# A hybrid decoder layer with its activations kept channel-major, norms accumulated under the matmuls, and interleaved query tiles

## The reference

```python
a = rmsnorm(x, in_norm_g)
u, q, kc, vc, ks, vs, kw, vw, gates = split(a @ w_in)       # 1024, 1024, 6 x 256, 24 columns
q, kc, ks, kw = partial_rope(...)                           # first 32 of 128 head dims
y_pool = (trailing means over 2/4/8/16 tokens - u) @ pool_w * pool_scale
y_nsa = g0 * compressed_attention + g1 * selected_blocks + g2 * window_512
h = x + concat(y_pool, y_nsa) @ w_out
h = h + (silu(n(h) @ w_gate) * (n(h) @ w_up)) @ w_down      # width 5632
h = h + sigmoid(n(h) @ w_ple_gate) * (p @ w_ple_proj)
out = rmsnorm(h, final_norm_g)
```

## Time and profile before

| | us |
|---|---|
| median of 4 runs | 2118.09 (2095.25 to 2284.78) |
| the profiled execution | 2096.27, its span 2094.7 |
| TensorE busy | 1758.5 (84%) |
| VectorE / ScalarE / GpSimd busy | 642.9 / 454.7 / 65.9 |
| DMA | 159 MB moved, 76 GB/s over the span |

### The profile page before, as it was taken

One profiled execution on the slowest core, in us unless ns is written; L12 is line 12 of the kernel. 1 busy time (PEld: TensorE's weight loads), 2 busy tenths in 40 slices (PEclk: granted clock), 3 DMA queues, 4 the chain that ended last, 5 costly groups with the idle time before them and its releaser, 6 DMA issues.

```text
span 2094.7 us, 28609 instructions; the slowest of 8 cores (2078.4 to 2094.7 us)
## 1 busy us (share of the span) xinstructions
PE 1758.5 (84%) x10432; PEld 964.9 (46%) x10580; DVE 642.9 (31%) x1626; ACT 454.7 (22%) x788; POOL 65.9 (3%) x120
## 2 busy tenths in 40 slices
PE   1892999676777784987999999999999999995991
PEld 1782788333444451434444444444444444443440
DVE  2423543151666651224101211131102201135334
ACT  3323212130576670014000000000000000005113
POOL 0000000011000000000000000000000000000000
PEclk9995899885899996997999999999999999995996
DMA  8448233411000007613461633354451526035223
GB/s 217 129 71 190 52 62 62 71 31 32 1 2 1 2 1 175 167 25 76 81 116 25 120 62 69 73 100 82 81 101 31 111 43 129 14 56 131 46 46 160
DMA packets 23033, 159.35 MB, mean 76 GB/s; under 512 B 3696, under 2 KB 5104, under 8 KB 6256
## 3 DMA queue, kind: packets, MB, share of 16 engines
q0 software_dynamic: 15696, 118.00, 30.4%
q1 hardware_dynamic: 7200, 39.51, 5.4%
HBM read 267.12 MB, written 8.39 MB: 132 GB/s over the span
## 4 chain that ended last, share of the span: by engine, by line
PE 78%; DVE 8%; DMA 7%; issue 4%; ACT 3%; DVEq 0%; SPq 0%; POOL 0%; ACTq 0%; POOLq 0%
PE ps L937 14%; PE ps L940 14%; PE ps L953 14%; PE ps L434 11%; PE ps L872 5%; PE ps L1001 5%; PE ps L542 3%; DMA arena<-x 2%; PE ps L720 2%; PE ps L711 2%; DMA arena<-wU 2%; PE ps L708 1%; PE ps L646 1%; DVE arena L910 1%; DVE arena L686 1%
## 5 line engine op out<-in xcount | busy, mean ns | idle before, releaser
L937 PE MATMUL ps<-arena 128*128 128x512 bf16 x1380 | 317.4, 380 | 1.6 <-issue 0.2
L940 PE MATMUL ps<-arena 128*128 128x512 bf16 x1380 | 316.1, 379 | 1.5
L953 PE MATMUL ps<-arena 128*128 128x512 bf16 x1379 | 303.0, 379 | 1.5
L434 PE MATMUL ps<-arena 128*128 128x256 bf16 x2048 | 239.2, 274 | 0.0
L944 DVE TENSOR_TENSOR arena<-ps,arena 128x512 bf16<-128x512 f32 x88 | 60.9, 692 | 548.2 <-PE ps L937 325.5
L943 ACT ACTIVATE arena<-ps 128x512 f32<-128x512 f32 x88 | 52.5, 597 | 782.6 <-PE ps L937 686.5
L937 PEld LDWEIGHTS ps<-arena 128*128 128x128 bf16 x1408 | 138.1, 98 | 166.9 <-issue 1.7
L940 PEld LDWEIGHTS ps<-arena 128*128 128x128 bf16 x1408 | 137.8, 98 | 166.1
L953 PEld LDWEIGHTS ps<-arena 128*128 128x128 bf16 x1408 | 137.7, 98 | 166.2
L434 PEld LDWEIGHTS ps<-arena 128*128 128x128 bf16 x2048 | 196.1, 98 | 23.9
L713 ACT ACTIVATE arena<-ps 128x512 bf16<-128x512 f32 x280 | 161.7, 597 | 85.7 <-PE ps L720 54.9
(11 more groups left out here) (139 smaller groups left out, 1157.9 us busy)
## 6 DMA issues: line engine op xcount, KB each, us to landing
arena<-x SPq DMA_DIRECT2D x24, 1024.0 KB, 12.4
arena<-wdown POOLq DMA_DIRECT2D x16, 1536.0 KB, 15.7
arena<-wgate POOLq DMA_DIRECT2D x22, 1024.0 KB, 9.1
arena<-wup POOLq DMA_DIRECT2D x22, 1024.0 KB, 11.9
arena<-wT POOLq DMA_DIRECT2D x16, 1024.0 KB, 9.5
arena<-wU POOLq DMA_DIRECT2D x8, 1024.0 KB, 10.7
arena<-wout POOLq DMA_DIRECT2D x4, 2048.0 KB, 17.9
arena<-wpg POOLq DMA_DIRECT2D x4, 2048.0 KB, 13.7
```

The costliest lines, as they stand in the source:

```text
L434: PE(lambda e, dc=dc: e.matmul(ps[pbank][:, 0:256], lhsT=aT[:, dc, i * 128:(i + 1) * 128], rhs=wsl[wi][:, dc, :], start=(dc == 0), stop=(d ...
L937: PE(lambda e, dc=dc, sl=sl, half=half, th2=th2, pg=pg: e.matmul(ps[pg][:], lhsT=wgu[sl][:, dc, half * 128:(half + 1) * 128], rhs=a2T[:, d ...
L940: PE(lambda e, dc=dc, sl=sl, half=half, th2=th2, pu=pu: e.matmul(ps[pu][:], lhsT=wgu[sl + 1][:, dc, half * 128:(half + 1) * 128], rhs=a2T[ ...
L953: PE(lambda e, ci=ci, ot=ot, sl=sl, pb=pb, ncq=ncq: e.matmul(ps[pb][:], lhsT=hT[:, ci, ot * 128:(ot + 1) * 128], rhs=wdn[sl][:, ci, :], st ...
```

## The change

The kernel is written anew around the same matmuls.

- Layout: `x`, `p` and the output are handed over channel-major, so channels are on the partitions from the start. The norm's sum over channels is then a sum over partitions: `stat` squares each 128-channel chunk on ScalarE and adds it up on VectorE, `rs` sums over partitions with one float32 matmul by a matrix of 1/2048 and takes the power -1/2 as Exp(-0.5 Ln), `scaled` multiplies. No norm has a transpose.
- Tokens: a core's own tiles are every other tile of the sequence (`OWN`, the odd ones in its numbering) instead of one half; the other core of the sequence has the rest. Local tile 0 is padding on one of the two.
- Projections run over four blocks of 512 tokens (two of other tiles, two of own). All six K and V slabs stay in SBUF (`wkv`). K is projected channel-major and needs no transpose; rotary is done on channel-major data. The norm of block b + 1 is interleaved as `tasks` with the chunks of block b. Q follows for the two own blocks, still held in `aT`.
- Compression: its weights are loaded during the projections, and ScalarE copies K and V into an order in which the stride becomes contiguous (`relay`), one copy after each chunk of Q. Pooling: the halo of 16 tokens is now needed at each tile (128 columns for each channel chunk).
- Attention: a chain at own tile `ot` has 2 `ot` + 2 steps of the selected branch and 2, 4 or 5 of the window; the chains go by `ot`, both groups after each other. The mask matmul and the choice of blocks are left out for `ot` < 4. Masking by `wvalid` goes. All four slots of `wout` are loaded during attention.
- The residual is channel-major. The statistics of the next norm are accumulated in the loops that finish it, and the norm of the first half of the tokens is emitted after the second half's first group. FFN quarters are 12, 12, 12 and 8 chunks.

The core of the diff:

```diff
-        hgs = [4, 5, 6, 7, 8, 9] if pas == 0 else list(range(10))
...
-            ltq = 8 + ot
...
+OTHER = np.arange(0, 16, 2)
+OWN = np.arange(1, 16, 2)
+ORDER = np.concatenate([OTHER, OWN])
...
+            gt = _tiles(th)[ORDER]
+            xl = np.zeros((16, 128, 2048), F)
+            xl[gt >= 0] = x[b].reshape(16, 128, 2048)[gt[gt >= 0]]
+            m["x"] = _c(xl.reshape(4, 512, 16, 128).transpose(0, 3, 2, 1).reshape(4, 128, 16 * 512))
...
+    def stat(src, B_src, i, first, hold=False):
+        a, Ba = acc[i]
...
+        q, Bq = sq[sqr()]
+        ACT(lambda e: e.activation(out=q, in_=src, func=AF.Square), [B_src], [Bq])
+        flush(i)
+        late[i] = lambda: DVE(lambda e: e.tensor_tensor(out=a, in0=a, in1=q, op=ALU.add), [Ba, Bq], [Ba])
...
+    def rs(i, pb):
+        flush(i)
+        a, Ba = acc[i]
+        r, Br = rsb[i]
+        PE(lambda e: e.matmul(ps[pb][:], lhsT=ones, rhs=a, start=True, stop=True), [B_ones, Ba], [PB[pb]])
+        ACT(lambda e: e.activation(out=r, in_=ps[pb][:], func=AF.Ln, bias=eps), [PB[pb], B_eps], [Br])
+        ACT(lambda e: e.activation(out=r, in_=r, func=AF.Exp, scale=-0.5), [Br], [Br])
+
+    def scaled(dst, B_dst, src, B_src, which, dc, i):
+        DVE(lambda e: e.scalar_tensor_tensor(out=dst, in0=src, scalar=gv[:, which, dc:dc + 1], in1=rsb[i][0], op0=ALU.mult, op1=ALU.mult),
+            [B_src, B_gv, rsb[i][1]], [B_dst])
...
         for dc in range(16):
+            tasks.append(lambda dc=dc: stat(*src(dc), b % 2, dc == 0))
+        tasks.append(lambda: rs(b % 2, bank()))
+        for dc in range(16):
+            tasks.append(lambda dc=dc: scaled(aT[b % 2][:, dc, :], B_aT[b % 2][dc], *src(dc), 0, dc, b % 2))
...
+        ACT(lambda e: e.activation(out=dst[64:128], in_=src[64:128].rearrange("p (a b) -> p a b", a=4), func=AF.Copy), [PB[pb]], B_dst)
+        DVE(lambda e: e.tensor_tensor(out=u1[0:64], in0=src[0:64], in1=tab[0:64, 0, :], op=ALU.mult), [PB[pb], Bt], [B1])
+        DVE(lambda e: e.tensor_tensor(out=u2[0:16], in0=src[32:48], in1=tab[32:48, 1, :], op=ALU.mult), [PB[pb], Bt], [B2])
+        DVE(lambda e: e.tensor_tensor(out=u2[32:48], in0=src[0:16], in1=tab[0:16, 1, :], op=ALU.mult), [PB[pb], Bt], [B2])
+        DVE(lambda e: e.tensor_tensor(out=dst[0:64], in0=u1[0:64].rearrange("p (a b) -> p a b", a=4), in1=u2[0:64].rearrange("p (a b) -> p a b", a=4), op=ALU.add),
+            [B1, B2], B_dst)
...
+    for t in x_tasks(0):
+        t()
+    for b in range(4):
+        tasks = x_tasks(b + 1) if b < 3 else []
+        n_done = 0
+        steps = [lambda i=i, t=t: v_chunk(b, t, i) for i in (4, 5) for t in range(4)]
+        steps += [lambda i=i, g=g: kv_chunk(b, i, g) for i in (1, 0, 2, 3) for g in range(2)]
+        upto = [1, 3, 5, 7, 9, 11, 13, 15, 16, 20, 24, 28, 31, 99, 99, 99]
+        for k, f in enumerate(steps):
+            f()
+            while len(tasks) > 0 and n_done < upto[k]:
+                tasks.pop(0)()
+                n_done += 1
...
+                    ACT(lambda e: e.activation(out=cP[k][:, g, :].rearrange("p (h n) -> p h n", h=16)[:, :, n * 32:(n + 1) * 32],
+                                               in_=cT[k][:, g, n * 512:(n + 1) * 512].rearrange("p (n h) -> p h n", h=16), func=AF.Copy), [B_cT[k]], [B_cP[k]])
+                relay.append(piece)
...
+        mm(pb, ps[pb][:, 0:254].rearrange("p (g n) -> p g n", g=2), [(w_[:, l, :], cP[kv][:, :, (l % 16) * 128 + l // 16:(l % 16) * 128 + l // 16 + 127]) for l in range(32)], lambda l: [Bw, B_cP[kv]])
...
+    WO = [R4, R4 + 16 * KB, R5, R5 + 16 * KB]
+    wo = [tile(f"wo{i}", WO[i], [16, 512], BF16) for i in range(4)]
+    for i in range(4):
+        load("pool", f"wo{i}", flat(wo[i][0]), wout_d[i], wo[i][1])
...
+        topk = ot >= 4
...
+        lt = 2 * ot + 1
+        win = [k for k in range(lt - 4, lt + 1) if k >= 0]
+        todo = [(1, k, k == 0, k == lt) for k in range(lt + 1)] + [(2, k, k == win[0], k == lt) for k in win]
...
+                p, Bp = score_exp(k_[:, g, kt * 128:(kt + 1) * 128], B_kT[br - 1][g][kt], g, ot, kt if (br == 1 and ot >= 4) else None)
+                m = diag if last else (upst if (br == 2 and kt == lt - 4) else None)
+                if m is not None:
...
+            mm(pb, ps[pb][:], [(w_[:, c, j * 128:(j + 1) * 128], ymixT[:, c, h * 512:(h + 1) * 512]) for c in range(16)], lambda c: [Bw, B_ym[c][h]])
+            add_h(pb, h, dm, True)
+            if h == 1 and dm == 0:
+                norm(0, 1)
+    gus = [load_gu(0), load_gu(1)]
...
+                    if first_group:
+                        first_group = False
+                        norm(1, 1)
...
+                    down(h, dm // 4, dm % 4)
+                    if h == 1 and dm == 0:
+                        norm(0, 2)
...
+    def final(h):
+        rs(h, bank())
+        for dc in range(16):
+            scaled(hT[h][:, dc, :], B_h[h][dc], hT[h][:, dc, :], B_h[h][dc], 3, dc, h)
+            if dc % 2 == 1:
+                ob = S.buf(f"out{h}{dc}")
+                S.dma("sp", lambda e, dc=dc: e.dma_start(out=out_d[h, :, (dc - 1) * 512:(dc + 1) * 512], in_=hT[h][:, dc - 1:dc + 1, :].rearrange("p a b -> p (a b)")),
```

More of the change, by code:

```diff
@@ new lines, in build, with mm, const @@
+    bank = Rot(8)
+    def mm(pb, out, pairs, reads, skip=False):
+        n = len(pairs)
+        for i, (lhsT, rhs) in enumerate(pairs):
+            PE(lambda e, i=i, lhsT=lhsT, rhs=rhs: e.matmul(out, lhsT=lhsT, rhs=rhs, start=(i == 0), stop=(i == n - 1)), reads(i), [PB[pb]])
+    off = [R0]
+    def const(name, shape, dtype=F32):
+        n = int(np.prod(shape)) * (2 if dtype == BF16 else 4)
+        v = tile(name, off[0], shape, dtype)
+        off[0] += (n + 31) // 32 * 32
+        return v
@@ new lines, in run_with @@
+    def run_with(tasks, steps, first=0):
+        n = len(steps) - first
+        done = 0
+        for k, s in enumerate(steps):
+            s()
+            want = len(tasks) * max(0, k + 1 - first) // n
+            while done < want:
+                tasks[done]()
+                done += 1
+    for t in x_tasks(0):
[11 more added lines that the diff above has]
+                n_done += 1
@@ new lines, in pv, with c1_stages @@
+    def pv(p, Bp, rhs, B_r, width, obanks, first, last):
+        for r in range(4):
+            bk, c0 = obanks[r // 2], (r % 2) * 256
+            PE(lambda e, r=r, bk=bk, c0=c0: e.matmul(ps[bk][:, c0:c0 + width], lhsT=p[:, r, :], rhs=rhs, start=(first and r % 2 == 0), stop=last, skip_group_check=True),
+               [Bp, B_r], [PB[bk]])
+    chains = [(ot, g) for ot in range(8) for g in range(2)]
+    deferred = []
+    def c1_stages(ci):
+        ot, g = chains[ci]
+        p, Bp = PTc[ci % 2]
+        (ib, Bi), (iw, Biw), (m, Bm), (sel, Bsel) = imp[ci % 2]
+        topk = ot >= 4
+        def s0():
+            sb = srot()
+            PE(lambda e: e.matmul(ps[sb][:], lhsT=kcmpT[:, g, :], rhs=q_of(g, ot), start=True, stop=True), [B_kcmp, B_qT[g][ot]], [PB[sb]])
+            ACT(lambda e: e.activation(out=flat(p), in_=ps[sb][:], func=AF.Exp, scale=SCALE), [PB[sb]], [Bp])
+            DVE(lambda e: e.tensor_tensor(out=p, in0=p, in1=bcast4(cvalid[:, ot * 128:(ot + 1) * 128]), op=ALU.mult), [Bp, B_cvalid], [Bp])
@@ L842, in build @@
+    LA = 2
+    live = {}
+    for i in range(len(steps) + LA):
+        if i < len(steps):
+            if steps[i][2] is not None:
+                steps[i][2]()
+            live[i] = steps[i][0]()
+        if i >= LA:
+            steps[i - LA][1](live.pop(i - LA))
+        for d in list(deferred):
+            d[0] -= 1
+            if d[0] <= 0:
+                deferred.remove(d)
+                d[1]()
     while deferred:
         deferred.pop(0)[1]()
[L844 removed]
@@ new lines, in norm, with load_gu @@
+    def norm(h, which):
+        rs(h, bank())
+        for dc in range(16):
+            scaled(a2T[h][:, dc, :], B_a2[h][dc], hT[h][:, dc, :], B_h[h][dc], which, dc, h)
+    wgu = [[tile(f"wgu{i}{k}", WO[i] + k * 8 * KB, [16, 256], BF16) for k in range(2)] for i in range(2)]
+    wgi = Rot(2)
+    def load_gu(grp):
+        i = wgi()
+        load("pool", f"wgu{i}0", flat(wgu[i][0][0]), wg_d[grp], wgu[i][0][1])
+        load("pool", f"wgu{i}1", flat(wgu[i][1][0]), wu_d[grp], wgu[i][1][1])
+        return wgu[i]
```

1403 lines of the change are left out of this document (578 added, 825 removed).

## The result

The changed kernel takes 1810.8 us in the median of ten runs, beside 2097.5 for the kernel before (sixteen runs); the ratio is 0.8634, with a 95% interval of 0.8625 to 0.8643. The forecast was 1755 with a range of 1700 to 1850: the direction and the range hold, and the time is 56 us above the point. It also lies above the 1710 to 1800 that the forecast gave itself without the rivals. The profiled execution has a span of 1807.4 us against 2095 before.

A forecast was written before the change was run, and what follows sets the result against it. TensorE's program order, broken by norms and cold loads, was taken as the bound. Stages 38 + 225 + 9 + 79 + 218 + 110 + 921 + 127 + 22 = 1749, plus 1.6 is 1751, named 1755 us; range 1700 to 1850.

The forecast's parts named there:

- rival of an attention that doesn't shrink: Attention stays at the old 274 us through waits of 3.2 us a chain; total 1807 us; chance 0.08.
- The clock rival: Dense stages: TensorE held below full clock, total 167 + 1584/c us for mean clock c; chance 0.10.
- The projections: Four blocks of 512 tokens, 170 us with gates and sums, plus Q at 55: 225 us, was 309.
- the last slab is wanted at 73: Projections: block 1's x and five slabs, loading from 23 us on, are done by 67, before the last slab's need.
- Eight banks hide 14 us: Projections: PSUM copies stand behind a ScalarE square waiting for x; eight PSUM banks hide 14 us of that.
- rival of late loads: First blocks: a late slab or x, 6.5 us per late slab, five of them 33; total 1784 us; chance 0.06.
- it is covered, barely: Projections: VectorE's 37 us a block, 40 with gaps, stays under TensorE's 41.6.
- The VectorE rival: VectorE bounds the projections at 50 us a block, costing 8.4 x 4 there; total 1800 us; chance 0.08.
- Attention, +17.6: Attention with fewer steps and masks: 218 us, between 195 (no waits) and 250 (half clock for short chains).
- The long chains: Attention, ot 4 to 7: step prices plus 4 x (0.8 + 3.2) for compressed branch and waits, 63 us per group.
- The short chains: Attention, ot 0 to 3: VectorE sets a floor of 9.5, 9.5, 10.8 and 12 us a chain, 42 per group.
- Signs of being wrong: TensorE waiting for scaled writes at block starts, short chains over 14 us each, or a dense stage's clock under 1.00.

The follow-up runs named there:

- split_half: Changed kernel with attention's old step counts, mask and block choice in every chain (output not the reference's): 1854.2 us, ratio 0.8846; attention 280.7 us.
- xf_norot: Changed kernel with three weight slabs issued after block 1's x, and rotary arithmetic replaced by one ScalarE copy (output not the reference's): 1788.6 us, ratio 0.8529.
- all three edits: Changed kernel with three slabs issued after block 1's x, the compressed branch at later steps, and pooling groups reversed: 1782.6 us, ratio 0.8492.

## Why the prediction was right, and where it was not

**What held.** The path is TensorE's program order, and what was cut from it came off the time: the 71 us between the projection passes, the stride of the compression's gather, `wout`, and the norms of FFN and end. Compression at 9.0 and pool at 79.3 are the predicted numbers to a few tenths, with the wait ahead of the last pooling output at 8.2 for 8.5. FFN and gate stage are 3 us over their 1048. Attention has its 216 Exp and lost 38 us of 274, so that the rival of an attention that doesn't shrink falls; split_half gives the reason, 45 us for the interleaving. The last quarter lost 5 us (1.89 + 0.51 + 2.46 + 0.24 of TensorE's idle time) where I said 8.

**The clock rival.** FFN: 886.7 us at a granted 1.00, the 2.4 GHz level, with all eight cores at work. The Trainium skill (TensorE: Matmul & The Clock Gate, "Seeing it yourself") has 13/16 for dense matmuls on three or more cores of a die; the row of this execution does not agree, as that of before did not the earlier trace rows.

**The projections, +26.6.** The step that failed is the sentence "the last slab is wanted at 73". It looked for the deadline among the weights. The deadline of the same transfers is the sum for block 1, which stands in TensorE's own program some 21 us into block 0, about 65 us; with TensorE in order, everything behind it stands too. "Eight banks hide 14 us" speaks of copies and says nothing of this matmul. The size was off as well: 44 us of DMA from 23 on were to end at 67, and the engines stayed full until 75. That is the rival of late loads, with its mechanism right (`x` in the first blocks) and its price, 33 us, too high: the wait was 10.5, and the slabs themselves were never late. Taking it away gave 13 us. The second piece is "it is covered, barely". The busy time was right, 37.8 for 37, but a block also holds two stretches of waiting in series with it, 3.8 us each, the first all and the second about half for ScalarE. The joints cost 2.3 + 2.1 + 2.8 = 7.2 us in all, and xf_norot gave 8.8. The VectorE rival is right in its place, at a quarter of its price in the projections, 34. The remaining 6 to 9 us are blocks of 43.4 and 44.5 us without their joints for 42.5, and matmuls at the lower clock level after the wait (0.88 and 0.90 in the two stretches around it).

**Attention, +17.6.** The long chains were 126 in the sum and 130.9 in the trace of the slowest core, but 126.8 on five of the other seven. Their price took the distance of the old chains, with the compressed branch where it used to stand; the change moves it forward, to where the window branch of the chain before still has the banks. I read the list of steps and priced no wait for it. With the branch put back they take 123.3. So where the clock is near full the price was met with the wait in it, by a balance that the sum did not work out, and the excess on the slowest core goes with a granted clock of 0.88, 0.90 and 0.96 in its third to fifth long chain. The short chains were 84 and 4 to begin, and are 103.3. Two of them hold most of that: the first, 20.8 with what leads to it, against 13.5, and the eighth, 18.4 against 12. Sub-stretches of the changed kernel (table of stages):

```profile
382.60:403.40 20.80, 10.92 (x54) 5.76 (x54) 12.60 (x49) 9.25 (x16) 1.91 (x4) 0.50 1.00 172
...
467.40:485.90 18.50, 13.11 (x81) 8.03 (x80) 11.15 (x48) 8.75 (x17) 0.00 (x0) 0.68 0.00 1
```

In the first TensorE is busy 10.9 us at the 1.2 GHz level, with 9.7 us of waits for the first compressed branches. The clock does not set this chain: from its first score to its cast it takes 20.97 us at a granted 0.50, and 20.98 at 0.66 with the pooling groups reversed; with the late branch it takes 20.43 at 0.50, and 20.43 at 0.67 with all three edits. In the eighth the selection for the first long chain runs, with the waits of TensorE on VectorE that belong to it, at a mean clock of 0.68. Here the clock goes with some 2 us: the eighth chain takes 18.4 us on the two cores where it is 0.69 and 16.5 on the two where it is 0.89, still far from 12. With all three edits the short chains take 99.2 us of the 88 priced. What sets the rest of this part was not tried and stays open.

**Start and small terms.** First projection matmul at 34.5 us for 31: the first sum stands at 29.9, its float32 matmul takes 2.05 and what follows until the first scaled write 2.5. The sixteen scaled writes pace TensorE at 0.66 us each for 0.62. Output projection, +4: 1.6 of it are idle time of TensorE (112.7 busy in 114.3). Two slips of the sum change nothing: the matmuls of the clock rival add up to 1583 and not 1584, and the bare 32 in the pool's sum are matmuls, 6.9 us.

**Signs of being wrong.** All three that the prediction named showed, each in a part of its place: TensorE waits for scaled writes at each block's start (2.3, 2.1 and 2.8 us), two of the eight short chains take over 14 us, and the clock is 0.88 to 0.96 in the first projection blocks. That the time is inside the range all the same is owed to the width that the rivals gave it.

## What to carry to other kernels

When work is moved under an in-order engine, look for its deadline on every engine that waits for it, small matmuls of a norm included: here 4 MB of `x` were due before the weights that were issued ahead of them. A cover of 37 us under 42 is none if two waits of 4 us stand in series with it; count the chain through the other engines, not the busy time alone. And a moved step can wait for a resource that its old place had left free (moving the compressed branch back gave 11 us, in part the wait for its PSUM banks); a list of step numbers in a diff deserves a sentence in the sum. Before a low clock is blamed for a slow stretch, compare the same stretch on cores or in runs with another clock: the first chain took 21.0 us at 0.50 and at 0.66.

## What the runs showed of the hardware

A float32 matmul of 128x512 stands in the traces as two instructions, listed with 1.02 us where TensorE came out of dense work and 2.05 after a wait. What counts beside the 0.2157 of a bf16 matmul of 512 columns is the time from start to start: 0.85 us after dense work (115.43 to 116.28 in `xf_norot`), about four times as much, and 1.84 after the wait of 10.5 us (75.54 to 77.38 in the changed kernel). A megabyte took 22.7 (`x`) and 26.9 us (slabs) to land while two queues shared the sixteen engines, each taking about half, and 13.8 for `x` in the median of the whole execution. GpSimd adds two 128x512 float32 tiles in 1.26 us, 1.4 with its gap, against 0.69 on VectorE.
